# Layer 1's sums begin with rows that GpSimd weighs, and the gate's row is fetched first

## The chip, the cores and the metric

The kernel runs on one core of one Trainium2 chip. The metric is the time of one execution on the device, in microseconds; three executions give the median. Engine names are those of the profile: PE is TensorE, DVE is VectorE, ACT is ScalarE, POOL is GpSimd, SP issues the DMAs.

## The reference

Two layers of a transformer over 1024 tokens (plus 256 context tokens in layer 0), width 1024. Each layer has a mixer (attention), a projection `w_out`, a gated residual with layer norm, and a squared-ReLU MLP with a second gated residual:

```
x = _layer_norm(DEEPNORM_ALPHA * x + g_a * y, ln1_g[l], ln1_b[l])
x = _layer_norm(DEEPNORM_ALPHA * x + g_m * _squared_relu_mlp(x * (1 + sc_m) + sh_m, mlp_w1[l], mlp_w2[l]),
                ln2_g[l], ln2_b[l])
```

So the MLP's sum of a row starts from ALPHA times the normalised, weighted and shifted row: `ALPHA * (xhat * ln1_g + ln1_b)`. The gate `g_a` is one row of 1024 numbers for all tokens (and another for the context).

## The kernel before

`stage_block(layer)` holds projection, first norm and MLP of one layer. Tokens are in tiles of 128: ten in layer 0, eight in layer 1 (`final`). Each engine has its own instruction list and works it off in order; semaphores tie the lists together.

**Projection.** For each tile PE makes 48 matmuls (L2250 to L2252: each fp32 product is three products of split halves) into a pair of PSUM banks. DVE then multiplies by the gate row (L2077, two halves), adds the residual (L2084), takes moments (L2087, L2090), and normalises (L2096); ACT gives the square root between. PE transposes the normalised tile (L2235) after the sixth of the eight k-steps of the *next* tile, so it stands still if the normalised tile is late. In layer 1 the residual tile `r_xin` is x-hat of layer 0's end, and POOL first multiplies it by `r_lng` and adds `r_lnb` (L1972, L1974); L2084 waits for that (`s_past`). In layer 0 POOL's use of these two rows (L1979, L1981) is behind the transposes. SP issues, once the split of `w_out` is done: `r_lng`, `r_lnb` (L1788), the gate row or rows (L1790), the first residual tiles (L1776), then the next `r_raw`. The two rows and the gate rows count on one semaphore `s_row` (three transfers in layer 1, four in layer 0), and both POOL and DVE wait for all of them.

**Start of layer 1's MLP.** The MLP runs in steps of 256 hidden columns. In a step PE makes the first product for two groups of 512 tokens (L2295 to L2297, two column blocks m each), ACT takes ReLU and square (L1947, L1949), POOL squares the ReLU in full precision (L2000), DVE makes the low half (L2163). One step later PE makes the second product (L2273 to L2275) and DVE adds it to the sum `y` (L2106). In layer 1 POOL also multiplies the second weights by the MLP's gate (L1993) and makes the low half of the next first weights (L1987), ACT and DVE split the second weights (L1940, L2156). Before any sum, `begin_y` loads row tile t of `y` (the stored x-hat) and makes it `ALPHA*(y*ln1_g + ln1_b)` by two DVE operations, L2039 and L2041; `r_over` are the two broadcast rows `ln1`. Tile 0 is begun before the split of the last transposed tile (L2025, which PE needs for group 1), tiles 1 to 7 in step 0's second group. PE's wait for the first second product is

```
wait(pe, s_y, tiles + nth(c, t) - 1)
```

With `tiles` = 8 and c = t = 0 that is 7: seven row tiles must be begun, and for t = 1 all eight. PE also waits there for the low halves of group 0 and of the second weights.

Of the kernel before, what the change touches and what calls it, by code (L numbers as in the profile page):

```python
# [19 lines left out]
P = 128  # L20
# [1633 lines left out]
def stage_block(nc, io, k, layer):  # L1654
# [30 lines left out]
    rsem = lambda n: k.sem(f"{rtag}_{n}")  # L1685
    s_row, s_xr, s_past, s_begin = rsem("rows"), [rsem(f"x{i}") for i in range(XB)], rsem("past"), rsem("begin")
    s_raw = [rsem(f"raw{i}") for i in range(2)]
    s_whigh, s_wlow, s_high, s_low, s_yps = [rsem(x) for x in ("whigh", "wlow", "high", "low", "yps")]
    s_dve, s_std, s_g, s_b, s_tr, s_mod, s_hh, s_hl, s_half = [rsem(x) for x in ("dve", "std", "g", "b", "tr", "mod", "hh", "hl", "half")]
    s_lnr, s_lnt, s_fold = rsem("lnr"), rsem("lnt"), rsem("fold")  # L1690
    s_store = [rsem(f"store{i}") for i in range(2)]
# [67 lines left out]
    with nc.Block() as block:  # L1759
        @block.sync  # L1760
        def _(sp):
# [22 lines left out]
            for i, name in enumerate(("ln1_g", "ln1_b")):  # L1784
                sp.dma_start(lnr[i * KT:(i + 1) * KT, :], io[name][layer].rearrange("(k p) -> k p", p=P)).then_inc(s_lnr, 16)
            sp.wait_ge(s_wlow, KT)
            for t, name in ((lng, "ln2_g"), (lnb, "ln2_b")) if final else ((lng, "ln1_g"), (lnb, "ln1_b")):
                sp.dma_start(t[:, :], bass.AP(tensor=io[name].tensor, offset=0, ap=[[0, P], [1, D]])).then_inc(s_row, 16)  # L1788
            for c in range(3 - XB):
                sp.dma_start(rgate[:, c, :].rearrange("p (j q) -> p j q", q=P),  # L1790
                             bass.AP(tensor=k.gate_dram.tensor, offset=(layer * 2 * 2 * KT + c) * P, ap=[[0, P], [2 * P, KT], [1, P]])).then_inc(s_row, 16)
            for t in range(XB):
                residual_in(t)
            for t in range(tiles):
                if t + 2 < tiles:
# [170 lines left out]
        def _(pool):  # L1966
            k.clear_last(pool)
            pool.wait_ge(s_row, 48 if final else 64)
            for t in range(tiles) if final else ():
# [5 lines left out]
            for t in () if final else range(tiles):  # L1975
# [5 lines left out]
                pool.tensor_tensor(r, r, lnb[:, :], ALU.add).then_inc(s_b, 1)  # L1981

            def step(c):
                for m in range(M):
                    if not starts(c):
                        wait(pool, s_ahigh, M * c + m + 1)
                        pool.tensor_tensor(wal[:, m, :, :], rawa[:, m, :, :], f32(wah[:, m, :, :]), ALU.subtract).then_inc(s_alow, 1)  # L1987
                if final:
                    for m in range(M):
                        if starts(c):  # L1990
                            pool.wait_ge(s_grow, 16)
                        wait(pool, s_rawb[m], 16 * (c + 1))
                        pool.tensor_tensor(rawb[:, m, :], rawb[:, m, :], growt, ALU.mult).then_inc(s_bg, 1)  # L1993
                for g, (a, n) in enumerate(groups):
                    for m in range(M):
                        j = J * c + g * M + m
                        wait(pool, s_relu, j + 1)
                        wait(pool, s_atl, j - 1)
                        r = rel[:, m % 2, 0:n]
                        pool.tensor_tensor(sq[:, m % 2, 0:n], r, r, ALU.mult).then_inc(s_sq, 1)  # L2000
                    if ends(c) and not final:
                        for t in (range(4), range(4, 6), range(6, tiles))[g]:
# [11 lines left out]
        def _(dve):  # L2014
# [17 lines left out]
            def begin_y(first, end):  # L2032
                for t in range(first, end):
                    if final:
                        dve.wait_ge(s_yx[t], 16)
                        y = by_j(k.y[:, t, :])
                        if t == 0:
                            dve.wait_ge(s_begin, 32)
                        dve.scalar_tensor_tensor(out=y, in0=y, scalar=ALPHA, in1=ln1[0], op0=ALU.mult, op1=ALU.mult).then_inc(s_past, 1)  # L2039
                        dve.wait_ge(s_past, 2 * tiles + t + 1)  # L2040
                        dve.scalar_tensor_tensor(out=y, in0=ln1[1], scalar=ALPHA, in1=y, op0=ALU.mult, op1=ALU.add).then_inc(s_y, 1)  # L2041
                    else:
# [18 lines left out]

            dve.wait_ge(s_row, 48 if final else 64)
            for t in range(tiles):
# [7 lines left out]
                if t >= 2:  # L2071
                    dve.wait_ge(s_store[t % 2], 16 * (t // 2))
                    dve.wait_ge(s_tr, t - 1)
                dve.wait_ge(s_yps, t + 1)
                for half in range(2):
# [66 lines left out]
            def step(c):  # L2142
# [6 lines left out]
                for g, (a, n) in enumerate(groups):  # L2149
# [3 lines left out]
                    if g == NG - 1:  # L2153
                        for m in range(M):
                            wait(dve, s_bhigh, M * c + m + 1)
                            dve.tensor_tensor(wbl[:, m, :], rawb[:, m, :], f32(wbh[:, m, :]), ALU.subtract).then_inc(s_blow, 1)  # L2156
                        if final and starts(c):
                            begin_y(1, tiles)
                    for m in range(M):
                        j = J * c + g * M + m  # L2160
                        wait(dve, s_sq, j + 1)
                        wait(dve, s_ath, j + 1)
                        dve.tensor_tensor(atl[:, m, a:a + n], sq[:, m % 2, 0:n], f32(ath[:, m, a:a + n]), ALU.subtract).then_inc(s_atl, 1)  # L2163
            def ending_first(c):
                def low(g, m):
# [232 lines left out]
```

## Time and profile before

| | us |
|---|---|
| median of 3 runs | 2968.99 |
| lowest, highest | 2968.83, 2974.59 |
| profiled execution, device time | 2971.22 |
| its span, first to last instruction | 2969.4 |
| PE busy (share of the span) | 2793.5 (94%) |
| DVE, ACT, POOL busy | 1367.4, 887.6, 533.5 |
| mean granted clock of TensorE | 0.973 |

PE is the bound: a wait of PE is time lost, a wait of another engine costs only where PE waits for it in turn. In the rows, "idle before" with an arrow names what ended the idle time. A duration of DVE or POOL includes the time in which the operation has started but makes no progress. The projection of layer 0 begins at about 499 us of the span, that of layer 1 at about 2117 us, layer 1's MLP at about 2229 us.

### The profile page before, as it was taken

How to read it: one execution, taken by the hardware profiler on the slowest of the kernel's cores; microseconds unless marked ns; L12 is line 12 of the kernel's file. 1: busy time of each engine (PE TensorE's matmuls, PEld its weight loads, DVE VectorE, ACT ScalarE, POOL GpSimd, SP SyncE). 2: the span in 40 equal slices, each digit the busy share in tenths (PEclk: the TensorE clock that was granted, in tenths of full speed). 3: DMA queues.
4: the chain of work that ended last, by engine and by line, in shares of the span. 5: the costliest groups of instructions: out<-in, count | busy, mean ns of one | idle time of the engine just before them, and what ended most of it. 6: DMA issues, size and time to landing. Idle time of an engine off the chain costs nothing. (4 is left out here: it accounts for less than half of the span.)

```text
span 2969.4 us, 40552 instructions
## 1 busy us (share of the span) xinstructions
PE 2793.5 (94%) x15615; PEld 2289.2 (77%) x15615; DVE 1367.4 (46%) x2195; ACT 887.6 (30%) x1598; POOL 533.5 (18%) x365
## 2 busy tenths in 40 slices
PE   6999996999999999999969999999697999999998
PEld 3666785788888888888858888888585888888886
DVE  3575554663333333333573565555556333333336
ACT  3244653441211211211132443444342211221222
POOL 0000000341121121111320000000133323323321
PEclk8999998999999999999989999999898999999999
DMA  7584216440010110110331111100455111111112
GB/s 260 189 309 149 75 63 225 123 133 29 29 56 28 39 46 28 42 42 28 85 114 50 36 44 37 36 29 15 129 141 149 57 42 42 57 42 42 57 42 57
DMA packets 202132, 237.42 MB, mean 80 GB/s; under 512 B 15960, under 2 KB 165088, under 8 KB 195872
## 3 DMA queue, kind: packets, MB, share of 16 engines
q1 hardware_dynamic: 201728, 235.74, 24.9%
q8 instruction: 78, 1.28, 0.2%
q14 instruction: 38, 0.31, 0.0%
q10 hardware_dynamic: 288, 0.10, 0.0%
HBM read 203.20 MB, written 36.83 MB: 81 GB/s over the span
## 5 line engine op out<-in xcount | busy, mean ns | idle before, releaser
L2106 DVE TENSOR_TENSOR y<-y,pair 128x1024 f32<-128x1024 f32 x280 | 341.7, 1221 | 337.4 <-PE pair L2275 337.4
L2273 PE MATMUL pair<-m_wbh,m_ath 128*128 128x512 f32 x1080 | 422.1, 391 | 16.8 <-DVE y L2041 16.8
L2275 PE MATMUL pair<-m_wbh,m_atl 128*128 128x512 f32 x1080 | 423.2, 392 | 0.0
L2274 PE MATMUL pair<-m_wbl,m_ath 128*128 128x512 f32 x1080 | 422.2, 391 | 0.0
L1947 ACT ACTIVATE m_rel<-pair 128x512 f32<-128x512 f32 x160 | 88.9, 556 | 1021.0 <-PE pair L2297 1009.9
L2163 DVE TENSOR_TENSOR m_atl<-m_sq,m_ath 128x512 fp32r<-128x512 f32 x150 | 96.4, 644 | 623.1 <-POOL m_sq L2000 623.1
L2000 POOL TENSOR_TENSOR m_sq<-m_rel 128x512 f32<-128x512 f32 x160 | 155.5, 972 | 1124.7 <-ACT m_rel L1947 1124.5
L2297 PE MATMUL pair<-hth,m0n_wal 128*128 128x512 f32 (+1 forms) x768 | 272.2, 354 | 0.0
L2296 PE MATMUL pair<-htl,m0n_wah 128*128 128x512 f32 (+1 forms) x768 | 272.1, 354 | 0.0
L2295 PE MATMUL pair<-hth,m0n_wah 128*128 128x512 f32 (+1 forms) x768 | 271.6, 354 | 0.0
L2273 PEld LDWEIGHTS pair<-m_wbh,m_ath 128*128 128x128 f32 x1080 | 203.4, 188 | 60.7 <-issue 16.3
L2275 PEld LDWEIGHTS pair<-m_wbh,m_atl 128*128 128x128 f32 x1080 | 203.3, 188 | 43.3
L2274 PEld LDWEIGHTS pair<-m_wbl,m_ath 128*128 128x128 f32 x1080 | 203.3, 188 | 43.2
L2295 PE MATMUL pair<-hth,m1n_wah 128*128 128x512 f32 x512 | 200.0, 391 | 3.3 <-DVE htl L2025 3.3
L2296 PE MATMUL pair<-htl,m1n_wah 128*128 128x512 f32 x512 | 200.4, 391 | 0.0
L2297 PE MATMUL pair<-hth,m1n_wal 128*128 128x512 f32 x512 | 200.4, 391 | 0.0
L2296 PEld LDWEIGHTS pair<-htl,m0n_wah 128*128 128x128 f32 x768 | 145.1, 189 | 21.6
L2295 PEld LDWEIGHTS pair<-hth,m0n_wah 128*128 128x128 f32 x768 | 145.1, 189 | 21.1
L2297 PEld LDWEIGHTS pair<-hth,m0n_wal 128*128 128x128 f32 x768 | 145.1, 189 | 20.1
L1496 DVE CUSTOM_DVE_ANT_0 a_sx<-pair,a_tab 128x640 f32<-128x640 f32 (+1 forms) x128 | 96.0, 788 | 86.7 <-PE pair L1588 86.7
L2250 PE MATMUL pair<-r_wh,r_cath 128*128 128x512 f32 x288 | 116.5, 404 | 6.1 <-DVE r_catl L2020 5.0
L1940 ACT ACTIVATE m_wbh<-m_rawb 128x1024 fp32r<-128x1024 f32 x60 | 60.3, 1053 | 194.7 <-PE pair L2275 194.7
(284 smaller groups left out, 5283.7 us busy)
## 6 DMA issues: line engine op xcount, KB each, us to landing
a_ring<-in_w_mod SPq DMA_DIRECT2D x40, 1024.0 KB, 9.4
m_rawb<-in_mlp_w SPq DMA_DIRECT2D x64, 512.0 KB, 4.4
m_rawa<-in_mlp_w SPq DMA_DIRECT2D x60, 512.0 KB, 4.1
x_rows<-r_res SPq DMA_DIRECT2D x26, 512.0 KB, 5.4
r_raw<-cat_cols SPq DMA_DIRECT2D x18, 512.0 KB, 6.4
mod_w<-in_w_mod SPq DMA_DIRECT2D x8, 1024.0 KB, 12.2
r_xin<-in_x SPq DMA_DIRECT2D x16, 512.0 KB, 12.4
gate_pre<-a0g_gout SPq DMA_DIRECT2D x20, 256.0 KB, 2.0
```

The costliest lines, as they stand in the source:

```text
L1496: dve.tensor_tensor_reduce(sx[:, n % 2, hh, 0:keys], two[:, at:at + keys], table(hh, t), -1.0, 3.0e38, ALU.add, ALU.min, sm[:, 0:1]).then_ ...
L1947: act.activation(rel[:, m % 2, 0:n], k.bank[4 + jj % NB1][:, 0:n], ACT.Relu).then_inc(s_relu, 1)
L2000: pool.tensor_tensor(sq[:, m % 2, 0:n], r, r, ALU.mult).then_inc(s_sq, 1)
L2106: dve.tensor_tensor(k.y[:, t, :], k.y[:, t, :], k.pair[t % 2][:, :], ALU.add).then_inc(s_y, 1)
L2163: dve.tensor_tensor(atl[:, m, a:a + n], sq[:, m % 2, 0:n], f32(ath[:, m, a:a + n]), ALU.subtract).then_inc(s_atl, 1)
L2250: pe.matmul(o, cath[:, t % 2, kt, :], wh[:, kt, n], start=kt == 0, stop=False)
L2273: pe.matmul(o, ath[:, m, ts], bh[:, m, cols], start=m == 0, stop=False)
L2274: pe.matmul(o, ath[:, m, ts], bl[:, m, cols], start=False, stop=False)
L2275: i = pe.matmul(o, atl[:, m, ts], bh[:, m, cols], start=False, stop=m == M - 1)
L2295: pe.matmul(o, wah[:, m, kt, :], xh, start=kt == 0, stop=False)
L2296: pe.matmul(o, wah[:, m, kt, :], xl, start=False, stop=False)
L2297: i = pe.matmul(o, wal[:, m, kt, :], xh, start=False, stop=kt == KT - 1)
```

## The change

It has two parts.

**The fetches.** SP issues the gate row of condition 0 first, then the first residual tile, then `r_lng` and `r_lnb`, then the rest. The gate rows have semaphores of their own (`s_rg`). DVE no longer waits for `s_row`; it waits for the gate row at each tile, right before L2077. POOL waits for `r_lng` and `r_lnb` (and in layer 1 for the residual tile, as before).

**The begin of layer 1's sums.** The product `y * ln1_g` of all eight tiles goes from DVE to POOL (`weigh`): tiles 0 to 2 at the start of step 0, ahead of POOL's products of the second weights; tiles 3 and 4 behind its second square, tile 5 behind the third, 6 and 7 behind the fourth. DVE multiplies the row `ln1_b` by ALPHA once, and keeps one operation per tile, `ALPHA*y + that row`. Its tiles 1 to 4 now stand behind group 0's low halves and ahead of the split of the second weights, tiles 5 to 7 behind group 1's low halves. What PE waits for is not changed.

```diff
             sp.wait_ge(s_wlow, KT)
+            gate_in(0)
+            residual_in(0)
             for t, name in ((lng, "ln2_g"), (lnb, "ln2_b")) if final else ((lng, "ln1_g"), (lnb, "ln1_b")):
                 sp.dma_start(t[:, :], ...).then_inc(s_row, 16)
-            for c in range(3 - XB):
-                sp.dma_start(rgate[:, c, :]..., ...).then_inc(s_row, 16)
-            for t in range(XB):
+            for t in range(1, XB):
                 residual_in(t)
+            for c in range(1, 3 - XB):
+                gate_in(c)
...
-            pool.wait_ge(s_row, 48 if final else 64)
+            pool.wait_ge(s_row, 32)
...
+            def weigh(t):
+                if t == 0:
+                    pool.wait_ge(s_begin, 32)
+                pool.wait_ge(s_yx[t], 16)
+                y = by_j(k.y[:, t, :])
+                pool.tensor_tensor(y, y, ln1[0], ALU.mult).then_inc(s_past, 1)
...
+                if starts(c) and final:
+                    for t in range(3):
+                        weigh(t)
...
                         pool.tensor_tensor(sq[:, m % 2, 0:n], r, r, ALU.mult).then_inc(s_sq, 1)
+                        if starts(c) and final:
+                            for t in ((), (3, 4), (5,), (6, 7))[g * M + m]:
+                                weigh(t)
...
-                        dve.wait_ge(s_yx[t], 16)
                         y = by_j(k.y[:, t, :])
                         if t == 0:
                             dve.wait_ge(s_begin, 32)
-                        dve.scalar_tensor_tensor(out=y, in0=y, scalar=ALPHA, in1=ln1[0], op0=ALU.mult, op1=ALU.mult).then_inc(s_past, 1)
+                            dve.tensor_scalar(ln1[1], ln1[1], ALPHA, None, ALU.mult).then_inc(s_shift, 1)
+                            dve.wait_ge(s_shift, 1)
                         dve.wait_ge(s_past, 2 * tiles + t + 1)
-                        dve.scalar_tensor_tensor(out=y, in0=ln1[1], scalar=ALPHA, in1=y, op0=ALU.mult, op1=ALU.add).then_inc(s_y, 1)
+                        dve.scalar_tensor_tensor(out=y, in0=y, scalar=ALPHA, in1=ln1[1], op0=ALU.mult, op1=ALU.add).then_inc(s_y, 1)
...
-            dve.wait_ge(s_row, 48 if final else 64)
...
+                dve.wait_ge(s_rg[cond(t)], 16)
                 dve.wait_ge(s_yps, t + 1)
...
-                        if final and starts(c):
-                            begin_y(1, tiles)
...
+                    if final and starts(c):
+                        begin_y(*((1, 5), (5, tiles))[g])
```

POOL's row at the start of layer 1's MLP before; the first line is the last residual tile, L1987 opens step 1:

```order
L1974 TENSOR_TENSOR r_xin<-r_xin,r_lnb 128x1024
L1993 TENSOR_TENSOR m_rawb<-m_rawb,y 128x1024 x2
L2000 TENSOR_TENSOR m_sq<-m_rel 128x512 x4
L1736 UNCONDITIONAL_BRANCH
L1736 ISA
L1987 TENSOR_TENSOR m1n_wal<-m_rawa,m1n_wah 128x1024
```

The same place after the change (L1994 is the weighing, L2009 the gated weights, L2016 the square, L2000 the low half of step 1):

```order
L1980 TENSOR_TENSOR r_xin<-r_xin,r_lnb 128x1024
L1994 TENSOR_TENSOR y<-y,r_over_15488 128x1024 x3
L2009 TENSOR_TENSOR m_rawb<-m_rawb,y 128x1024 x2
L2016 TENSOR_TENSOR m_sq<-m_rel 128x512 x2
L1994 TENSOR_TENSOR y<-y,r_over_15488 128x1024 x2
L2016 TENSOR_TENSOR m_sq<-m_rel 128x512
L1994 TENSOR_TENSOR y<-y,r_over_15488 128x1024
L2016 TENSOR_TENSOR m_sq<-m_rel 128x512
L1994 TENSOR_TENSOR y<-y,r_over_15488 128x1024 x2
L1737 UNCONDITIONAL_BRANCH
L1737 ISA
L2000 TENSOR_TENSOR m1n_wal<-m_rawa,m1n_wah 128x1024
```

Eight operations of 128x1024 have come into POOL's row ahead of step 1, three of them ahead of the gated weights and the first square.

DVE's row before, from the last tile's normalisation on (L2025 is the split of the last transposed tile, L2163 the low halves, L2156 the split of the second weights); six more pairs L2039, L2041 follow, then L2163 twice:

```order
L2096 TENSOR_SCALAR r_res<-r_res,r_mv,r_rstd 128x1024
L2039 SCALAR_TENSOR_TENSOR y<-y,r_over_15476 128x1024
L2041 SCALAR_TENSOR_TENSOR y<-r_over_15476,y 128x1024
L2025 TENSOR_TENSOR htl<-r_modt,hth 128x8x128
L2163 TENSOR_TENSOR m_atl<-m_sq,m_ath 128x512 x2
L2156 TENSOR_TENSOR m_wbl<-m_rawb,m_wbh 128x1024 x2
L2039 SCALAR_TENSOR_TENSOR y<-y,r_over_15476 128x1024
```

DVE's row after, up to the end of step 0:

```order
L2115 TENSOR_SCALAR r_res<-r_res,r_mv,r_rstd 128x1024
L2057 TENSOR_SCALAR r_over_15488<-r_over_15488 128x8x128
L2060 SCALAR_TENSOR_TENSOR y<-y,r_over_15488 128x1024
L2044 TENSOR_TENSOR htl<-r_modt,hth 128x8x128
L2180 TENSOR_TENSOR m_atl<-m_sq,m_ath 128x512 x2
L2060 SCALAR_TENSOR_TENSOR y<-y,r_over_15488 128x1024 x4
L2175 TENSOR_TENSOR m_wbl<-m_rawb,m_wbh 128x1024 x2
L2180 TENSOR_TENSOR m_atl<-m_sq,m_ath 128x512 x2
L2060 SCALAR_TENSOR_TENSOR y<-y,r_over_15488 128x1024 x3
```

Sixteen begin operations have become eight and one scaling; four of them now stand ahead of the split of the second weights, and the last three behind both remaining low halves.

SP's row in layer 0 before, from the norm's weights to the third cat tile:

```order
L1785 DMA r_lnr<-in_ln_b 8x128
L1788 DMA r_lng<-in_ln_g 128x1024
L1788 DMA r_lnb<-in_ln_b 128x1024
L1790 DMA r_gate<-gate_rows 128x8x128 x2
L1776 DMA r_xin<-in_x 128x1024
L1766 DMA r_raw<-cat_cols 128x8x128
```

The same after:

```order
L1786 DMA r_lnr<-in_ln_b 8x128
L1789 DMA r_gate<-gate_rows 128x8x128
L1777 DMA r_xin<-in_x 128x1024
L1795 DMA r_lng<-in_ln_g 128x1024
L1795 DMA r_lnb<-in_ln_b 128x1024
L1789 DMA r_gate<-gate_rows 128x8x128
L1767 DMA r_raw<-cat_cols 128x8x128
```

The gate's first row has moved from third to first place, the residual tile from fifth to second. In layer 1 the order changes in the same way, with one gate row and a second residual tile in its place.

## Rows read from the trace of the kernel before

**Rows 1.** The page: busy time and share of the span of each engine
```profile
PE 2793.5 (94%) x15615; PEld 2289.2 (77%) x15615; DVE 1367.4 (46%) x2195; ACT 887.6 (30%) x1598; POOL 533.5 (18%) x365
```

**Rows 2.** Waits of PE, 2105 to 2300 us (us in all, times, longest)
```profile
PE pair L2273 <- DVE y L2041: 16.8, 2, 15.9
PE pair L2235 <- DVE r_res L2096: 11.9, 2, 11.0
...
PE pair L2295 <- DVE htl L2025: 3.3, 1, 3.3
```

**Rows 3.** Timeline of POOL, 2138 to 2152 us (start, us, operation, idle before)
```profile
2140.86 2.34 POOL L1972 TENSOR_TENSOR r_xin<-r_xin,r_lng 128x1024 f32<-128x1024 f32 x1 [81.54 <-DMA r_xin<-x_rows]
...
2145.58 2.34 POOL L1972 TENSOR_TENSOR r_xin<-r_xin,r_lng 128x1024 f32<-128x1024 f32 x1
2147.99 3.20 POOL L1974 TENSOR_TENSOR r_xin<-r_xin,r_lnb 128x1024 f32<-128x1024 f32 x1
```

**Rows 4.** Timeline of DVE, 2138 to 2152 us
```profile
2145.72 3.27 DVE L2084 SCALAR_TENSOR_TENSOR r_res<-r_xin,r_res 128x1024 f32<-128x1024 f32 x1 [5.16 <-POOL r_xin L1974]
```

**Rows 5.** Timeline of DVE, 2238 to 2284 us
```profile
2240.79 1.45 DVE L2039 SCALAR_TENSOR_TENSOR y<-y,r_over 128x1024 f32<-128x1024 f32 x1 [6.00 <-DMA y<-x_rows]
...
2243.41 1.22 DVE L2025 TENSOR_TENSOR htl<-r_modt,hth 128x1024 fp32r<-128x1024 f32 x1
...
2261.66 1.22 DVE L2039 SCALAR_TENSOR_TENSOR y<-y,r_over 128x1024 f32<-128x1024 f32 x1
...
2266.45 3.37 DVE L2039 SCALAR_TENSOR_TENSOR y<-y,r_over 128x1024 f32<-128x1024 f32 x1
...
2276.44 3.28 DVE L2041 SCALAR_TENSOR_TENSOR y<-r_over,y 128x1024 f32<-128x1024 f32 x1
```

**Rows 6.** Timeline of POOL, 2235 to 2280 us
```profile
2236.39 4.76 POOL L1993 TENSOR_TENSOR m_rawb<-m_rawb,y 128x1024 f32<-128x1024 f32 x2 [19.05 <-DMA m_rawb<-in_mlp_w]
...
2258.16 1.24 POOL L2000 TENSOR_TENSOR m_sq<-m_rel 128x512 f32<-128x512 f32 x1 [4.39 <-ACT m_rel L1947]
2265.69 6.33 POOL L1987 TENSOR_TENSOR m1n_wal<-m_rawa,m1n_wah 128x1024 fp32r<-128x1024 f32 x2 [6.28 <-ACT m1n_wah L1923]
2271.98 6.66 POOL L1993 TENSOR_TENSOR m_rawb<-m_rawb,y 128x1024 f32<-128x1024 f32 x2
```

**Rows 7.** Timeline of PE, 2238 to 2284 us
```profile
2244.69 0.69 PE L2295 MATMUL pair<-hth,m1n_wah 128*128 128x512 f32 x1 [3.28 <-DVE htl L2025]
...
2273.33 0.79 PE L2273 MATMUL pair<-m_wbh,m_ath 128*128 128x512 f32 x1 [15.88 <-DVE y L2041]
...
2279.77 0.50 PE L2273 MATMUL pair<-m_wbh,m_ath 128*128 128x512 f32 x1 [0.96 <-DVE y L2041]
```

**Rows 8.** Tile y on SP, 2246.5 to 2249.5 us: issue to landing
```profile
DMA to landing us min/median/max: 5.0/6.6/11.4
```

**Rows 9.** Timeline of DVE, 514 to 524 us
```profile
517.70 1.28 DVE L2077 TENSOR_TENSOR r_res<-pair,r_gate 128x512 f32<-128x512 f32 x2
519.02 1.23 DVE L2084 SCALAR_TENSOR_TENSOR r_res<-r_xin,r_res 128x1024 f32<-128x1024 f32 x1
...
522.37 0.81 DVE L2096 TENSOR_SCALAR r_res<-r_res,r_mv,r_rstd 128x1024 f32<-128x1024 f32 x1
```

**Rows 10.** Timeline of PE, 518 to 530 us
```profile
523.24 1.97 PE L2235 MATMUL pair<-kept_ident,r_res 128*128 128x128 f32 x8 [4.65 <-DVE r_res L2096]
```

**Rows 11.** Windows: us, then PE busy (x), PEld, DVE, ACT, POOL, PEclk, DMA, GB/s
```profile
523.20:527.90 4.70, 4.66 (x15) 4.08 (x16) 1.14 (x1) 2.66 (x8) 2.44 (x2) 0.50 0.41 119
2273.30:2278.80 5.50, 5.47 (x12) 3.84 (x12) 5.46 (x2) 0.00 (x0) 5.34 (x2) 0.50 0.33 94
```

**Rows 12.** Timeline of SP, 505 to 530 us
```profile
507.77 0.36 SPq L1788 DMA_DIRECT2D r_lng<-in_ln_g  x1
```

**Rows 13.** DMA issues, 505 to 530 us (issue to landing in us)
```profile
r_lng<-in_ln_g SPq DMA_DIRECT2D x1, 512.0 KB, 4.5
r_lnb<-in_ln_b SPq DMA_DIRECT2D x1, 512.0 KB, 5.5
```

More of the change, by code:

```diff
@@ L1685, in stage_block @@
     rsem = lambda n: k.sem(f"{rtag}_{n}")
-    s_row, s_xr, s_past, s_begin = rsem("rows"), [rsem(f"x{i}") for i in range(XB)], rsem("past"), rsem("begin")
+    s_row, s_xr, s_past, s_begin, s_shift = rsem("rows"), [rsem(f"x{i}") for i in range(XB)], rsem("past"), rsem("begin"), rsem("shift")
     s_raw = [rsem(f"raw{i}") for i in range(2)]
@@ L1689, in stage_block @@
     s_dve, s_std, s_g, s_b, s_tr, s_mod, s_hh, s_hl, s_half = [rsem(x) for x in ("dve", "std", "g", "b", "tr", "mod", "hh", "hl", "half")]
+    s_rg = [rsem(f"rgate{c}") for c in range(2)]
     s_lnr, s_lnt, s_fold = rsem("lnr"), rsem("lnt"), rsem("fold")
@@ L1786, in _, with gate_in @@
             sp.wait_ge(s_wlow, KT)
+            def gate_in(c):
+                sp.dma_start(rgate[:, c, :].rearrange("p (j q) -> p j q", q=P),
+                             bass.AP(tensor=k.gate_dram.tensor, offset=(layer * 2 * 2 * KT + c) * P, ap=[[0, P], [2 * P, KT], [1, P]])).then_inc(s_rg[c], 16)
+            gate_in(0)
+            residual_in(0)
             for t, name in ((lng, "ln2_g"), (lnb, "ln2_b")) if final else ((lng, "ln1_g"), (lnb, "ln1_b")):
                 sp.dma_start(t[:, :], bass.AP(tensor=io[name].tensor, offset=0, ap=[[0, P], [1, D]])).then_inc(s_row, 16)
-            for c in range(3 - XB):
-                sp.dma_start(rgate[:, c, :].rearrange("p (j q) -> p j q", q=P),
-                             bass.AP(tensor=k.gate_dram.tensor, offset=(layer * 2 * 2 * KT + c) * P, ap=[[0, P], [2 * P, KT], [1, P]])).then_inc(s_row, 16)
-            for t in range(XB):
+            for t in range(1, XB):
                 residual_in(t)
+            for c in range(1, 3 - XB):
+                gate_in(c)
             for t in range(tiles):
```

## The prediction

> **What bounds the kernel now.** I read the page's busy shares first: PE is busy for 94% of the span and no other engine for half of it [rows 1]. So a change outside PE counts only by the waits of PE that it shortens or makes. Next PE's waits around layer 1's block [rows 2]: the longest of the stretch is 15.9 us for the begun sums (L2041, with a second of 0.96 us for the eighth tile), then 11.0 us for the first normalised tile, then 3.3 us for the split of the last transposed tile. In layer 0 PE waits 4.65 us for the first normalised tile [rows 10]. The change touches the first two of these places and the last.
>
> Then I looked at what DVE and POOL do while PE waits 15.9 us. DVE runs one begin operation behind another, and the same form takes 1.22 us at 2261.66 but 3.37 us at 2266.45 [rows 5]. The long ones begin where POOL starts its work for step 1: two low halves in 6.33 us and two gated weights in 6.66 us [rows 6], where the same gated weights took 4.76 us for two when DVE was idle. From 2266.45 to 2279.72 DVE got four operations done and POOL, within the same 13.27 us, about four. That is 3.32 us for one operation of each. POOL alone needs 2.38 us for one and DVE about 1.2: the two take turns, nothing runs side by side. The first tile shows the order of turns: POOL starts its next product at 2145.58, DVE's L2084 at 2145.72 takes 3.27 us, until 2148.99, and POOL's next, started at 2147.99, takes 3.20 us in its turn [rows 3, 4]. Sums that read PSUM are not among these operations.
>
> The Trainium skill has the rule for this in "SBUF — State Buffer", section "Who interferes with whom": a DVE instruction with two SBUF inputs and a GpSimd instruction that reads SBUF exclude each other, and whoever issued first holds the port for its whole length. It speaks against this change, which moves work to the engine that holds the port twice as long, and the trace agrees. What it leaves open is who comes next where both have a queue; rows 5 and 6 show turns. If POOL kept the port through its whole queue instead, DVE would start later, but the sum below is of all operations and would be no smaller.
>
> **Part 1, the fetches, layer 0.** The transfers of SP's queue land one after another: the first issued at 507.77 lands 4.5 us later, at 512.3; the second, issued some 0.4 us behind it, takes 5.5 us and lands near 513.7 [rows 12, 13]. All are of 512 KB. The gate row takes the first place and the residual tile the second, so L2077 can start near 512.5 and L2084 near 513.9. Before, L2077 starts at 517.70, L2084 at 519.02, and L2096 ends at 522.37 + 0.81 = 523.18 [rows 9]: 4.16 us from the start of L2084. The same chain now ends near 513.9 + 4.2 = 518.1. PE comes to the transposes at 523.24 - 4.65 = 518.6 [rows 10]. The wait goes: 4.65 us. Behind it the clock is at 0.50 (its lower level, 1.2 GHz) for 4.7 us [rows 11]; if PE never stands still it should not fall, and at full clock this stretch takes half: another 2.35 us. Sum 7.0 us. What is late next is the third cat tile, the sixth transfer in both orders: at 1.4 to 1.5 us per place it lands near 520, is split by ACT and DVE in about 2.3 us, and PE, through with the second tile at about 518.6 + 0.9 + 12 x 0.23 = 522.3, comes to it just then. I leave it at nothing. Two rows for POOL, `r_lng` and `r_lnb`, land later, but POOL first uses them behind the transposes. Bounds: if the gate's row lands one place later (1.4 us), PE waits about 1 us and gains 3.6 us without the clock; 7.0 is the other end.
>
> **Part 1, layer 1.** Here DVE's L2084 waits for POOL, and POOL needs the residual tile and both rows. These are four transfers with the gate's row, and the last of the four lands when it did: POOL starts at 2140.86 [rows 3]. The gate's product is earlier but L2084 waits 5.16 us for POOL [rows 4]. So the 11.0 us stay. Nothing, within 0.5 us either way.
>
> **Part 2, the begin of the sums.** Removed: eight DVE operations of 128x1024. Added: eight POOL operations of that size, at 2.38 us alone, and one scaling on DVE, at most as long as L2096 (0.81), hidden in the 6.00 us in which DVE waits for the first stored tile [rows 5]. PE still needs seven begun tiles. I count what has to go through the shared port before the seventh, from the landing of tile 0 (2240.8):
> - POOL, 128x1024: eight weighings, two gated weights of step 0 (before, these ran at 2236.39, in the gap; now they queue behind three weighings), and, as DVE's list is not through when POOL reaches step 1, two low halves and two gated weights of step 1. 14 operations. At 128x512: four squares.
> - DVE, 128x1024: the split L2025, two of the second weights, seven begins. 10 operations. At 128x512: four low halves.
>
> Ten pairs at 3.32 us are 33.2; four half-size pairs at 1.66 (half of it) are 6.6; the four operations that POOL has over at 2.38 are 9.5. Sum 49.3 us: the seventh tile is begun at 2290.1. The port has no gap on the way: the other five tiles are issued from 2246.44 on, land 5.0 to 11.4 us from their issue [rows 8], and their turns run from 2257 to 2274; the last square's input is there near 2263 (group 1's products took 2273.33 - 15.88 - 2244.69 = 12.8 us [rows 7], now from 2249.8 on), its turn is near 2269. Before, the seventh begin ended at 2266.45 + two pairs = 2273.1 and PE started 0.2 us later, at 2273.33 [rows 5, 7]. Now 2290.3, 17.0 us later. The second wait of 0.96 us [rows 7] goes, since the eighth begin follows one DVE operation later, inside the first tile's 5.5 us at half clock [rows 11]. Cost 16.0 us.
>
> On the way group 1 of PE's first product is late too. It waits for the split of the last transposed tile: weighing 0 until 2243.2, begin 0 in turn behind weighing 1 until 2246.5, the split behind weighing 2 until 2249.8, against 2243.41 + 1.22 = 2244.6. PE's 3.28 us [rows 7] become about 8.4. This does not add to the 16.0, as PE waits for the seventh tile in any case. What is queued behind POOL's weighings is the gated weights, then the squares; for these wait ACT's split of the weights and DVE's low halves, all of it inside the count.
>
> Bounds of this cost: if the five POOL operations that the seventh tile doesn't need (weighing 7, step 1's four) come after it, 11.9 us less: 4.1 us. Above, some 18 us, if a turn takes 2.42 us of POOL rather than 2.38 and each has a gap. I take 16.0, because the turns of rows 5 and 6 are of these very operations.
>
> **Sum.** -7.0 + 0 + 16.0 = +9.0 us. The profiled execution took 2971.22 us for a span of 2969.4; it would be 2980.2. The median of the runs shown is 2968.99, 2.2 us less, so 2978.0 us.
>
> **Rivals.**
> - *The turns let the seventh tile by.* If DVE passes POOL's last five operations, part 2 costs 4.1 us and the sum is -2.9: 2966 us, no change that can be told. For it: POOL's low halves of step 1 wait for weights, and these start only at 2265.69 [rows 6]. Against: that is long before their turn near 2278. 14%.
> - *No exclusion for the weighings.* This is the faster one. Place: step 0's start. If a weighing ran beside DVE's work, POOL alone would have done weighing 6 after 2240.8 + 9 x 2.38 (seven weighings and two gated weights) + 4 x 1.2 (a square, [rows 6]) = 2267.1, the begin ends at 2268.3, PE gains 4.8 + 0.96 us, and with layer 0's 7.0 the sum is -12.8: 2956 us. It decides as soon as DVE's begins take 1.2 us beside POOL's work. Rows 4 and 5 speak against it; for it only that no weighing has run yet. 10%.
> - *Layer 0 gives nothing.* The gate's row lands as small pieces and slow, or PE stands for the third cat tile instead. Then +16.0: 2985 us. The cat tile is not far from the edge (it is the sixth transfer in both orders). 10%.
>
> **How the numbers follow.** The forecast, both terms as worked out, has 66%; its own range is 2973 to 2982. A change within 0.2% (5.9 us) can't be told from none. Slower by more: nearly all of the forecast (0.61) and the third rival (0.10), 0.71. Same: the edge of the forecast (0.05) and the first rival, most of it (0.12), 0.17. Faster: 0.12. The range from 2966 to 2984 takes in the forecast, the first rival and part of the third, and leaves out the faster case.
>
> **What would show it.** Right: weighings of 3.2 to 3.4 us each in the timeline of POOL, begins of about 3.3 us on DVE with no idle time between, PE's first L2273 waiting 25 to 29 us and started near 2283 (7 us earlier by layer 0), PE's wait before group 1 near 8 us; in layer 0 L2235 of the first tile with no wait and the clock at 1.00 behind it; in layer 1's projection the 11.0 us unchanged. Wrong: begins of 1.2 us beside weighings; a wait of PE for L2273 under 16 us; a new wait of PE at layer 0's third tile; a first gate row that lands later than 514.

## The result, and the profile after

The changed kernel takes 2980.37 us (median of 9 runs) against 2970.58 us of the kernel before (9 runs): ratio 1.0031, interval 1.0022 to 1.0040. It is slower by 9.8 us. The forecast was 2978.0 us, +9.0 us.

The page of the changed kernel, first the span, then busy time and share of each engine:

```profile
span 2978.8 us, 40573 instructions
PE 2795.6 (94%) x15615; PEld 2291.0 (77%) x15615; DVE 1376.2 (46%) x2188; ACT 887.4 (30%) x1598; POOL 561.7 (19%) x373
```

PE is busy 2 us more than in [rows 1] and the span is 9.4 us longer, so the loss is waiting. The first and last records of PE's work in each stage cut both spans into the same pieces (start of the piece to start of the next, in us):

| stage | before | after | difference |
|---|---|---|---|
| start to layer 0's first projection product | 498.81 | 498.22 | -0.6 |
| to layer 0's last transposes | 131.81 | 126.01 | -5.8 |
| to layer 1's first projection product | 1486.84 | 1488.80 | +2.0 |
| to layer 1's last transposes | 117.38 | 117.53 | +0.2 |
| to the first second product (L2273, now L2292) | 38.49 | 53.86 | +15.4 |
| to the second tile's | 6.44 | 4.92 | -1.5 |
| to the end | 689.63 | 689.46 | -0.2 |
| sum | 2969.4 | 2978.8 | +9.4 |

The third stage (layer 0's MLP and both attentions) is work that the change doesn't touch. Among the profiles of all twelve kernels of this study it takes 1486.8 to 1488.8 us. The two kernels with the old fetches are at the low end, but so are three with the new ones, so no edit is shown to set it; with one profile per kernel the possibility isn't closed either. The first piece, ahead of every edit, differs even more, from 494.5 to 498.8 us. Differences of one or two us between whole spans of two profiles are therefore not read as an effect here, only those inside a stage.

PE's waits around layer 1's block (line, what it waited for: us in total, times, longest):

```profile
PE pair L2292 <- DVE y L2060: 25.2, 1, 25.2
PE pair L2254 <- DVE r_res L2115: 11.6, 2, 10.7
PE pair L2314 <- DVE htl L2044: 8.0, 1, 8.0
```

They answer to [rows 2]: the wait for the begun sums is 25.2 us instead of 15.9, that for the first normalised tile is 10.7 instead of 11.0, that for the last transposed tile's split is 8.0 instead of 3.3. POOL in that stretch (start, us, engine, line, out<-in, count of instructions; L1994 is the weighing, L2009 the gated weights, L2016 the squares, L2000 step 1's low half):

```profile
2236.05 7.94 POOL L1994 TENSOR_TENSOR y<-y,r_over 128x1024 f32<-128x1024 f32 x3 [22.84 <-DMA y<-x_rows]
2243.95 5.70 POOL L2009 TENSOR_TENSOR m_rawb<-m_rawb,y 128x1024 f32<-128x1024 f32 x2
2249.61 2.03 POOL L2016 TENSOR_TENSOR m_sq<-m_rel 128x512 f32<-128x512 f32 x2
2251.61 5.64 POOL L1994 TENSOR_TENSOR y<-y,r_over 128x1024 f32<-128x1024 f32 x2
2257.21 2.02 POOL L2016 TENSOR_TENSOR m_sq<-m_rel 128x512 f32<-128x512 f32 x1
2259.19 3.34 POOL L1994 TENSOR_TENSOR y<-y,r_over 128x1024 f32<-128x1024 f32 x1
2262.48 2.02 POOL L2016 TENSOR_TENSOR m_sq<-m_rel 128x512 f32<-128x512 f32 x1
2264.47 6.59 POOL L1994 TENSOR_TENSOR y<-y,r_over 128x1024 f32<-128x1024 f32 x2
2271.02 6.06 POOL L2000 TENSOR_TENSOR m1n_wal<-m_rawa,m1n_wah 128x1024 fp32r<-128x1024 f32 x2
2277.04 6.06 POOL L2009 TENSOR_TENSOR m_rawb<-m_rawb,y 128x1024 f32<-128x1024 f32 x2
```

No row but the first has idle time before it: from the landing of tile 0 at 2236.05 POOL works to 2283.10 without a gap. DVE beside it (L2060 begin, L2044 split of the transposed tile, L2180 low halves, L2175 split of the second weights):

```profile
2238.52 3.27 DVE L2060 SCALAR_TENSOR_TENSOR y<-y,r_over 128x1024 f32<-128x1024 f32 x1 [7.42 <-POOL y L1994]
2241.72 3.35 DVE L2044 TENSOR_TENSOR htl<-r_modt,hth 128x1024 fp32r<-128x1024 f32 x1
2250.68 4.32 DVE L2180 TENSOR_TENSOR m_atl<-m_sq,m_ath 128x512 fp32r<-128x512 f32 x2 [5.61 <-POOL m_sq L2016]
2254.92 10.66 DVE L2060 SCALAR_TENSOR_TENSOR y<-y,r_over 128x1024 f32<-128x1024 f32 x4
2265.51 6.63 DVE L2175 TENSOR_TENSOR m_wbl<-m_rawb,m_wbh 128x1024 fp32r<-128x1024 f32 x2
2272.06 5.57 DVE L2180 TENSOR_TENSOR m_atl<-m_sq,m_ath 128x512 fp32r<-128x512 f32 x2
2277.55 7.77 DVE L2060 SCALAR_TENSOR_TENSOR y<-y,r_over 128x1024 f32<-128x1024 f32 x3
```

In turn with a POOL operation of its own size, a DVE operation of 128x1024 takes about 3.3 us, as in [rows 5]. The four begins in 10.66 us are two such turns and two beside a square of half the size, 2.06 us each. The last begin of the last group starts when POOL is through and takes 1.2. PE's rows for the two waits, and its granted clock in the first tile of the second product and behind it (window, length, busy of PE, PEld, DVE, ACT, POOL, PEclk, DMA share, GB/s):

```profile
2245.12 0.79 PE L2314 MATMUL pair<-hth,m1n_wah 128*128 128x512 f32 x1 [8.00 <-DVE htl L2044]
2284.42 0.79 PE L2292 MATMUL pair<-m_wbh,m_ath 128*128 128x512 f32 x1 [25.23 <-DVE y L2060]
```

```profile
2284.40:2288.30 3.90, 3.88 (x9) 3.12 (x10) 0.92 (x1) 0.00 (x0) 0.00 (x0) 0.50 0.00 0
2288.30:2292.00 3.70, 3.70 (x16) 2.98 (x16) 1.22 (x1) 0.00 (x0) 0.00 (x0) 0.92 0.00 0
```

As in [rows 11], PE starts at 1.2 GHz (clock 0.50) after the wait. The second tile's first product follows at 2289.34 with no wait, so [rows 7]'s 0.96 us is gone.

In layer 0 the first tile's chain on DVE (L2096 the gate, L2103 the residual, L2115 the normalisation, L2039 the split of the third cat tile, that is of PE's input for the third tile, fetched from `cat_cols`) and PE's transposes and third tile:

```profile
511.66 1.29 DVE L2096 TENSOR_TENSOR r_res<-pair,r_gate 128x512 f32<-128x512 f32 x2 [1.40 <-DMA r_gate<-gate_rows]
513.22 1.23 DVE L2103 SCALAR_TENSOR_TENSOR r_res<-r_xin,r_res 128x1024 f32<-128x1024 f32 x1 [0.27 <-DMA r_xin<-in_x]
516.57 0.81 DVE L2115 TENSOR_SCALAR r_res<-r_res,r_mv,r_rstd 128x1024 f32<-128x1024 f32 x1
520.43 2.08 DVE L2039 TENSOR_TENSOR r_catl<-r_raw,r_cath 128x1024 fp32r<-128x1024 f32 x1 [3.04 <-ACT r_cath L1880]
```

```profile
517.81 1.03 PE L2254 MATMUL pair<-kept_ident,r_res 128*128 128x128 f32 x8
522.65 0.47 PE L2269 MATMUL pair<-r_wh,r_cath 128*128 128x512 f32 x1 [1.06 <-DVE r_catl L2039]
```

The 4.65 us of [rows 10] are gone and the clock of 500 to 545 us is 1.00 where it was 0.92. In their place stands 1.06 us for the third cat tile. In layer 1 DVE's L2103 still waits for POOL (8.80 us, until 2141.01), and POOL for the last of its transfers, as in [rows 3, 4]:

```profile
2136.14 2.35 POOL L1978 TENSOR_TENSOR r_xin<-r_xin,r_lng 128x1024 f32<-128x1024 f32 x1 [81.38 <-DMA r_lnb<-in_ln_b]
```

### The profile page after: what moved, and what is told of

Its sections match the earlier page's. It is cut to its first block and busy times, and to the rows that moved or that the text cites. A ratio compares the mean times of both kernels' runs of the same rounds, so it can differ in the third digit from the quotient of the medians.

```text
span 2978.8 us, 40573 instructions
## 1 busy us (share of the span) xinstructions
PE 2795.6 (94%) x15615; PEld 2291.0 (77%) x15615; DVE 1376.2 (46%) x2188; ACT 887.4 (30%) x1598; POOL 561.7 (19%) x373
## 5 line engine op out<-in xcount | busy, mean ns | idle before, releaser
L2292 PE MATMUL pair<-m_wbh,m_ath 128*128 128x512 f32 x1080 | 422.0, 391 | 25.2 <-DVE y L2060 25.2
L2180 DVE TENSOR_TENSOR m_atl<-m_sq,m_ath 128x512 fp32r<-128x512 f32 x150 | 103.6, 692 | 624.4 <-POOL m_sq L2016 624.4
L2016 POOL TENSOR_TENSOR m_sq<-m_rel 128x512 f32<-128x512 f32 x160 | 157.1, 983 | 1116.0 <-ACT m_rel L1953 1115.9
L2292 PEld LDWEIGHTS pair<-m_wbh,m_ath 128*128 128x128 f32 x1080 | 203.3, 188 | 68.4 <-issue 25.7
L2314 PEld LDWEIGHTS pair<-hth,m1n_wah 128*128 128x128 f32 x512 | 96.9, 189 | 29.1 <-DVE htl L2044 8.4
```

The source lines that it names most:

```text
L2292: pe.matmul(o, ath[:, m, ts], bh[:, m, cols], start=m == 0, stop=False)
L2314: pe.matmul(o, wah[:, m, kt, :], xh, start=kt == 0, stop=False)
```

## The experiments

Ten kernels, with 4 to 11 runs each beside the kernel before (medians 2970.0 to 2970.1 us in all three batches). Brackets are 95% intervals of the ratio. What was to be told apart: the two parts and whether they add; port against a mere queue; and where a better version lies.

**One part each.** The first kernel holds only the fetches, the second only POOL's weighings with DVE's new order of begins. The edits are the two halves of the diff above.

> Only the fetches (gate row first, residual tile second, gate waited for alone); the begin of layer 1's sums as before. Theory (the two parts add, the fetches help): in layer 0 the wait of 4.65 us for the first normalised tile goes, with the half clock behind it, less a wait of about 1 us for the third cat tile, as in the trace after: about 5.6 us faster, ratio 0.998. In layer 1's projection the 11 us stay. Rival (the gain of layer 0 is given back later): within 2 us of before, ratio 0.9995 or more.

> Only the weighing on POOL, with DVE's new order; the fetches as before. Theory (DVE and POOL take turns at a shared port, and all of the work goes through it): from the landing of stored tile 0 to PE's first second product 48.4 us as in the trace after, against 32.5 before, about 15 us slower than before, ratio 1.005. Rival (the two parts interact, and the weighing alone costs what the pair cost): about 9.8 us slower, ratio 1.0033.

The fetches alone take 2965.7 us, ratio 0.9987 [0.9978, 0.9996]: -4.3 us. The weighings alone take 2983.51 us, 1.0038 [1.0025, 1.0052]: +13.5 us. In us the intervals are -6.5 to -1.2 and +7.4 to +15.4. The sum of the two medians, +9.2, is the change's +9.8 within them: they add. PE's wait in the second kernel, in the first's place of [rows 2]:

```profile
PE pair L2286 <- DVE y L2054: 28.4, 1, 28.4
PE pair L2308 <- DVE htl L2038: 5.5, 1, 5.5
```

**A begin that doesn't read its second operand from SBUF.** If the port is the cause, a begin whose row comes from PSUM should pass POOL's work; if only POOL's list is too long, nothing changes.

```diff
-  dve.scalar_tensor_tensor(out=y, in0=y, scalar=ALPHA, in1=ln1[1], ...)
+  dve.scalar_tensor_tensor(out=y, in0=y, scalar=ALPHA, in1=by_j(k.pair[1][:, :]) if t else ln1[1], ...)
```

> The changed kernel, but the begins of tiles 1 to 7 add a PSUM tile instead of the row of ln1_b, so that each has one SBUF input only; this leaves out the shift of these rows. POOL's list is the same. Theory (turns at a port that only operations with two SBUF inputs and POOL use): a begin takes about 1.2 us beside a weighing, a weighing 2.4 to 2.6 us; seven begins leave the port, about 7 us of it before the seventh tile is begun; PE's first second product comes about 41 us after the landing of tile 0 instead of 48.4, so 6 to 8 us faster than the changed kernel, about 2973. Rival (POOL's longer queue alone is the cause, whatever DVE does): 48 us as before this edit, same time as the changed kernel, about 2980. A third: PSUM operands share the turns too, begins of 3.3 us and no change.

This kernel leaves out the row of `ln1_b` for seven tiles and adds whatever stands in that PSUM pair, so its output is of no use and only its time says something. 2967.03 us, 0.9988 [0.9979, 0.9997]: 3.0 us under before, where the changed kernel is 9.8 over, so 12.8 us less. DVE's begins, and PE's start:

```profile
2254.91 4.60 DVE L2060 SCALAR_TENSOR_TENSOR y<-y,pair 128x1024 f32<-128x1024 f32 x4
2269.04 3.47 DVE L2060 SCALAR_TENSOR_TENSOR y<-y,pair 128x1024 f32<-128x1024 f32 x3
```

```profile
2271.61 0.79 PE L2292 MATMUL pair<-m_wbh,m_ath 128*128 128x512 f32 x1 [13.03 <-DVE y L2060]
```

Four begins now take 4.60 us instead of 10.66, three 3.47 instead of 7.77, and the weighing beside the first four (2258.21) takes POOL's own 2.35. POOL's list is the same, and PE starts 35.6 us after tile 0's landing (2236.05 here too) instead of 48.4. So it is the exclusion, and "POOL's list alone" falls. Of a DVE instruction with at most one SBUF input, outside its 2-port modes, the section of the Trainium skill that the forecast quotes ("SBUF — State Buffer", "Who interferes with whom") says that it does not contend with GpSimd; the trace agrees, with four begins in 4.60 us. I had the size too small by half. The trace gives it: the seven begins take 10.36 us less (4.60 + 3.47 for 10.66 + 7.77), and the split of the second weights between them 4.20 instead of 6.63 us, 2.43 less, since it now runs beside the end of a weighing and a square. Together 12.8. I had priced the begins and not what stands behind them.

**The other way round: no weighings, begins earlier on DVE.** The last tile's split first, then the begins of tiles 0 to 2 at once instead of behind step 0's first products.

```diff
-            begin_y(0, 1 if final else XT)
-            split_ht(tiles - 1)
+            if final:
+                split_ht(tiles - 1)
+                begin_y(0, 3)
...
-                            begin_y(1, tiles)
+                            begin_y(3, tiles)
```

> The fetches, and no weighing on POOL: both begin operations stay on DVE, but the split of the last transposed tile goes ahead of begin 0, and tiles 1 and 2 are begun right behind it, in the time in which DVE stands idle before the first low half; tiles 3 to 7 as before. Theory (the seventh begin sets PE's start, and what counts is to have DVE's begins done before POOL reaches step 1 at about 2264): the seventh begin ends about 20 to 22 us after the landing of tile 0 instead of 32.5, PE starts 10 to 12 us earlier; with the fetches' 5.6 about 16 us faster than before, near 2955, ratio 0.9948. Rival (DMA landings of tiles 3 to 7 or the stores bound the begins): the gain beyond the fetches is under 5 us, 2960 to 2965.

2963.58 us, 0.9975 [0.9966, 0.9984]: -6.4 us, of which the fetches are 4.3. Much less than I expected. DVE:

```profile
2233.99 3.33 DVE L2031 TENSOR_TENSOR htl<-r_modt,hth 128x1024 fp32r<-128x1024 f32 x1 [5.21 <-ACT hth L1893]
2261.87 3.28 DVE L2047 SCALAR_TENSOR_TENSOR y<-r_over,y 128x1024 f32<-128x1024 f32 x1
2265.07 5.64 DVE L2173 TENSOR_TENSOR m_atl<-m_sq,m_ath 128x512 fp32r<-128x512 f32 x2
```

The split runs beside POOL's gated weights and takes 3.33 us, so that PE still waits 2.0 us for it; and the last begins and the last two low halves still meet POOL's step 1 (its low halves run from 2261.08 on). PE's wait for the sums falls from 15.9 to 10.8 us, and a new one comes behind it, for the first sum, which stands behind those low halves on DVE:

```profile
2260.93 0.79 PE L2283 MATMUL pair<-m_wbh,m_ath 128*128 128x512 f32 x1 [10.77 <-DVE y L2047]
2271.90 0.50 PE L2283 MATMUL pair<-m_wbh,m_ath 128*128 128x512 f32 x1 [2.96 <-DVE y L2116]
```

The size is that of my rival, but not its reason: no begin waited for a landing. DVE has no idle time from 2233.99 on, and the seventh begin ends at 2260.70, before POOL's step 1. So up to PE's start it is DVE's own list that counts, two operations per tile, and behind it the turns. What I missed is that DVE's whole list must be through before POOL starts step 1, not only the begins.

**The begin moved out of the stretch.** Where POOL has time is layer 1's projection: busy 19.74 of 48 us. There it can make `ALPHA*(y*ln1_g + ln1_b)` of each normalised tile in place, after PE's transposes and before the store, so that the row comes back as the begun sum. The first form does both operations on POOL; the second leaves the addition to DVE, one operation per tile (split first, tiles 0 to 2 early).

```diff
+            def row(t):                       # POOL, layer 1's projection
+                r = by_j(res[:, t % 2, :])
+                pool.wait_ge(s_dve, C * t + 6)
+                pool.wait_ge(s_tr, t + 1)
+                pool.tensor_tensor(r, r, ln1[0], ALU.mult).then_inc(s_g, 1)
+                pool.wait_ge(s_g, t + 1)
+                pool.tensor_tensor(r, r, ln1[1], ALU.add).then_inc(s_b, 1)   # first form only
...
+                        dve.tensor_tensor(y, y, ln1[1], ALU.add).then_inc(s_y, 1)   # second form only
```

> The fetches, and no begin at the MLP's start at all: during the projection, where POOL is busy for a fifth of the time, it multiplies each normalised tile by ALPHA*ln1_g and adds ALPHA*ln1_b behind its transposes (as it does in layer 0), the stored rows are the begun sums, and DVE only waits for their landing. Theory (the wait of 15.9 us is made of port work between the landing of the rows and step 1; taken from there it is gone): PE has no wait for begun sums, starts step 1 some 15 us earlier; POOL's added work takes turns with DVE in the projection, which may cost up to 1 us per tile in waits for L2096. About 2955, between 2950 and 2960, ratio 0.995. Rival (turns in the projection eat it): waits of PE for the normalised tiles of over 10 us more in all, 2962 or above.

> As e5_rows, but POOL only multiplies in the projection (one operation per tile), and DVE adds the row ALPHA*ln1_b at the MLP's start, one operation per tile, tiles 0 to 2 ahead of the first low half. Theory: half the port work at the MLP's start and half in the projection; PE still waits for the seventh begin, which ends about when its row lands (20 us after the landing of tile 0), so about 2957 to 2961, 2 to 5 us behind e5_rows. Rival (the projection is so near its limit that the second POOL operation costs more than the begins): faster than e5_rows.

The first takes 2957.91 us, 0.9960 [0.9947, 0.9974]: -12.1 us. The second takes 2951.23 us, 0.9932 [0.9918, 0.9945]: -18.8 us. So the order of the two is the other way round than I expected (the second 2 to 5 us behind the first): the rival named there came true. Cut into the pieces of the table above, the first form gains 20.0 us behind the last transposes (18.5 instead of 38.5) and loses 10.6 in layer 1's projection (128.0 instead of 117.4); the second gains 14.0 and loses 1.1. The fetches and the order of DVE's begins are the same in the second form as in the kernel with the early begins, which is at 0.9975; what moving the product alone brings is the rest, about 12 us.

The same 48 us of the projection in the first, in the second and (shifted by 5 us) in the kernel before:

```profile
2165.00:2213.00 48.00, 43.87 (x204) 35.78 (x203) 37.81 (x39) 18.89 (x39) 41.83 (x16) 1.00 0.40 111
```

```profile
2165.00:2213.00 48.00, 48.00 (x230) 40.05 (x229) 33.49 (x40) 21.69 (x47) 32.97 (x13) 1.00 0.52 143
```

```profile
2170.00:2218.00 48.00, 48.00 (x230) 40.03 (x229) 29.62 (x42) 21.73 (x45) 19.74 (x9) 1.00 0.56 160
```

With two operations per tile POOL is busy for 41.83 of the 48 us, DVE's operations queue for the port and PE stands for 4 of them; with one PE never stands. PE's waits of the first form and of the second:

```profile
PE pair L2259 <- DVE r_res L2118: 21.0, 8, 11.0
```

```profile
PE pair L2255 <- DVE r_res L2112: 12.8, 3, 11.7
PE pair L2293 <- DVE y L2053: 6.1, 1, 6.1
```

In the first form even the normalisation, which has one SBUF input of data, waits for POOL, 2.68 us instead of 0.81, in five of the eight tiles. One of them:

```profile
2226.11 2.68 DVE L2118 TENSOR_SCALAR r_res<-r_res,r_mv,r_rstd 128x1024 f32<-128x1024 f32 x1
```

**The 11 us of layer 1's projection.** The gate's row was never what ended it. This kernel has the fetches of the change, but in layer 1 the first residual tile comes first, then both rows, then the gate's row, and DVE scales the first tile itself; in layer 0 the third cat tile is fetched ahead of the norm's rows.

```diff
+            if not final:
+                cat_in(2)
...
+                if t == 0 and final:
+                    dve.wait_ge(s_row, 32)
+                    dve.wait_ge(s_xr[0], 16)
+                    x = xres[:, 0, :]
+                    dve.tensor_tensor(x, x, lng[:, :], ALU.mult).then_inc(s_own, 1)
+                    dve.wait_ge(s_own, 1)
+                    dve.tensor_tensor(x, x, lnb[:, :], ALU.add).then_inc(s_own, 1)
```

> e1_fetch, and for the first tile: in layer 1 the order is residual tile, its two rows, gate row, and DVE, which stands idle there, multiplies and adds for tile 0 instead of POOL; in layer 0 the third cat tile is fetched ahead of the two rows that POOL needs late. Theory: in layer 1 the 11 us wait shortens by one transfer (2.1 us), by 2.3 us of operations (two DVE instead of two POOL) and by the 2.2 us turn that L2084 loses to POOL: 5 to 6 us; in layer 0 the 1.06 us wait for the third cat tile goes. About 6 us faster than e1_fetch, 2959 to 2961. Rival (another transfer or the table of POOL's second tile becomes the bound): under 2 us faster than e1_fetch.

2958.13 us, 0.9962 [0.9948, 0.9975]: 7.6 us less than the fetches alone. The first tile's chain no longer has POOL's two operations in it and its L2106 meets no turn of POOL's (1.23 us, not 3.27). PE's wait is 4.8 us, where it is 12.8 in the profile of the fetches alone, 10.7 in the changed kernel and 11.0 before:

```profile
2130.66 1.23 DVE L2087 TENSOR_TENSOR r_xin<-r_xin,r_lng 128x1024 f32<-128x1024 f32 x1 [4.59 <-DMA r_lnb<-in_ln_b]
2134.38 1.23 DVE L2106 SCALAR_TENSOR_TENSOR r_res<-r_xin,r_res 128x1024 f32<-128x1024 f32 x1
```

```profile
PE pair L2257 <- DVE r_res L2118: 5.7, 2, 4.8
```

What the third cat tile is worth can be read in layer 0, where this kernel differs from the one with a single multiplication only by that fetch. PE comes to the first transposes 20.9 us into the projection in both; the other then waits 1.07 us for the third cat tile, this one doesn't, and the stage takes 126.0 instead of 127.4 us. So 1.4 of the 7.6 us are layer 0's, and the rest is the first tile's chain; the order of the fetches and DVE's two operations were not run apart.

**Together.** The order of the last kernel with each of the two forms before it.

> e5_rows and e7_first together. If they add: about 2949. If not (the first tile and the rows compete for the same transfers and turns): no better than e5_rows.

> e6_one and e7_first together: POOL's single multiplication in the projection, DVE's single addition at the MLP's start, and the first tile by DVE with the transfers in that order. The two shorten different waits, so they should add: e6_one is 18.8 us under before, e7_first 7.6 us under e1_fetch, which gives 26 us, about 2944, ratio 0.991. Rival: they share the transfers at the start, and it is no better than e8_all (2949.9).

With the first form 2949.89 us, 0.9925 [0.9911, 0.9938], 8.0 us under that form alone. With the second 2939.98 us, 0.9903 [0.9888, 0.9918]: 30.1 us under the kernel before (24.4 to 33.3 by the interval) and 40 under the changed one, the lowest median of the study; 26 us were expected from adding the two. What is left of the two waits:

```profile
PE pair L2309 <- DVE y L2060: 7.4, 1, 7.4
PE pair L2271 <- DVE r_res L2128: 5.8, 2, 4.9
```

**Is the wait for the begins needed at all?** PE's second product doesn't read `y`; only DVE's sum does. Here PE no longer waits for the begins, and DVE waits for all of them ahead of its first sum.

```diff
-                        dve.tensor_tensor(y, y, ln1[1], ALU.add).then_inc(s_y, 1)
+                        dve.tensor_tensor(y, y, ln1[1], ALU.add).then_inc(s_begun, 1)
...
+                            dve.wait_ge(s_begun, XT)
```

> e9_best, and PE no longer waits for seven and eight begins before the first two second products; only DVE waits for all begins before its first sum. Theory: PE's wait of 6.1 us for the seventh begin moves behind the second tile and becomes a wait for the first sum, which DVE can make at about the end of its low halves; what is gained is the two tiles' time less a longer half clock, 1 to 4 us under e9_best. Rival: the wait only changes its name, within 1 us of e9_best.

2943.28 us (4 runs), 0.9903 [0.9888, 0.9918]: not to be told from the kernel without the edit, whose median is 3.3 us lower at the same ratio. The gain of 1 to 4 us did not come; the rival did. PE starts two tiles (at 2242.58) and stands at the third, whose banks the first sum must free; DVE makes that sum only at 2251.50, behind its last begin, which waited for the last stored tile, and its low halves:

```profile
PE pair L2313 <- DVE y L2145: 4.4, 1, 4.4
```

```profile
2249.03 1.23 DVE L2060 TENSOR_TENSOR y<-y,r_over 128x1024 f32<-128x1024 f32 x1 [0.93 <-DMA y<-x_rows]
2251.50 2.34 DVE L2145 TENSOR_TENSOR y<-y,pair 128x1024 f32<-128x1024 f32 x2
```

The wait changed its name; the landing of the last stored tile and DVE's list behind it set it in both.

## Why the prediction was right

**The sum.** +9.0 us forecast, +9.8 [+6.5, +11.9] measured, and both terms of it have their own run.

**Layer 0: 7.0 forecast, 5.8 in the trace, 4.3 (1.2 to 6.5) in the run of that part alone.** The wait of 4.65 us and the half-clock stretch went as said (4.65 + 2.35). What came back is 1.06 us for the third cat tile, which I had named as next in line and set at nothing. It isn't nothing because the tile's split on DVE took 2.08 us, not 1.2 (it ran beside POOL's first product, started at 519.02), and because PE came for it at 521.59, not 522.3: the transposes started at 517.81, for which I had 518.6. The landing, at 519.33, was not late.

The 4.3 us of the single part are not apart from 5.8, as the interval shows, and its profile can't explain them: that execution took 2970.05 us, the longest of eleven with a median of 2965.7. What the profiles do show is that the gain depends on PE's clock at the start of the projection. In every kernel PE first stands for 7 to 10 us, runs ten matmuls, which begin at 0.50, and then stands 1.7 to 2.7 us for its first split. In some profiles the clock is at 1.00 when it goes on and stays there, in others it is at 0.50 for a part of the next 6 us. In the profiles of before and of the changed kernel the clock of 500 to 505 us is 1.00, in those of the two single parts 0.75 and 0.70. A PE that starts slower reaches the first tile's transposes later and waits less for them: 3.3 us in the kernel with the weighings alone, which has the old fetches, against 4.65. With the new fetches it then has no wait for the third cat tile. So like is to be compared with like: with the fast start the stage takes 131.8 us with the old fetches and 126.0 with the new ones, with a start of over 5 us at 0.50 it takes 132.4 (weighings alone) and 127.4 to 127.5 (begins from PSUM, fetches alone). The fetches are worth 5.8 us in the first case and 5.0 in the second. Which start the timed executions had is not known.

**Layer 1's projection: 0 forecast, +0.2 in the trace.** The wait is 10.7 instead of 11.0 us, and its end is POOL's, as [rows 3, 4] had it. The reordered kernel, with 4.8 us, shows that those transfers and POOL's operations together were the cause. From profile to profile this wait is not steady: with the same order of fetches it is 12.8 us in the one of the fetches alone, so "within 0.5 us" was too narrow.

**The begins: +16.0 forecast, 15.4 - 1.5 = 13.9 in the trace, +13.5 in the run of that part alone.** Steps that held: the weighings run without a gap from tile 0's landing; 14 operations of 128x1024 and 4 of 128x512 on POOL before the seventh begin is through; turns of 3.3 us for a pair of full size; PE's wait before group 1 8.0 us (8.4 forecast); its wait for L2292 25.2 (25 to 29 forecast); start at 2284.4 (2283 forecast); the second wait gone. The term that was mis-sized is the count of port time: 49.3 us forecast from the landing to the seventh begin, 48.1 measured (2236.05 to about 2284.1). The count of operations is right; about 0.7 of the 1.2 us are the four squares, 1.03 us each where the forecast's pairs hold 1.2. Another 0.5 us is the first tile's length, 4.92 us instead of 5.48, and a further 0.5 us that transposes and landing lie 5.5 us apart here, 5.95 before.

So the mechanism and the sizes held, but that the total is within 0.8 us is in part luck: layer 0 gave 1.2 us less than forecast and part 2 cost 2.1 us less, which nearly cancel, and the untouched stage between them was 2.0 us longer in this profile, for which no cause is shown. The medians of the single parts sum to +9.2.

**Rivals.** *The turns let the seventh tile by* fell: step 1's four POOL operations (2271.02 to 2283.10) ran in turns with DVE's last low halves and begins, before the seventh. *No exclusion for the weighings* fell by the same rows, and the begins that read PSUM show what the exclusion costs: 12.8 us of the changed kernel's time. That kernel is only 3.0 us faster than before, where this rival had 12.8, because its splits and low halves still take turns with POOL. *Layer 0 gives nothing* fell by the run of the fetches alone, though its interval reaches down to 1.2 us.

**What stays open.** Who gets the port next was only seen as turns; whether another order of the two lists would let DVE pass was not tried. What sets the level of PE's clock at the start of layer 0's projection was not tested, nor why the stage between the two projections takes up to 2.0 us more in some profiles.

## What to carry to other kernels

Where DVE and POOL both have lists of two-input SBUF work, count the operations of both together: a pair costs nearly the sum of both, here 3.3 us for 1.2 and 2.38, and moving one of DVE's two operations per tile to POOL made the stretch longer (+13.5 us). Move such work instead to a stretch where both have room, and count there too: the same product made by POOL in the projection before gave -18.8 us with the fetches and the earlier begins (about 12 of it its own), while two operations per tile filled POOL and gave only -12.1. When a wait is for several transfers, the order of the fetches helps only for the ones that the first user really needs: 4 to 6 us in layer 0, nothing in layer 1, where the gain came when the order and the work behind those transfers were changed together.

## What the runs showed of the hardware that I had not expected

- An operation of DVE with one input in SBUF and one in PSUM runs at its full pace beside POOL's 128x1024 products: 1.2 us each, with POOL's 2.35 us unchanged. The same operation with both in SBUF took 3.3.
- The normalisation (TENSOR_SCALAR, one SBUF input of data, 128x1024 in 0.81 us) did wait for POOL: 2.68 us, in five tiles of the kernel with both operations in the projection and in six of the one that adds the reordered start. That it reads one input doesn't free it.
- POOL's squares of 128x512 in turn with DVE's operations of 128x1024 took 2.02 us each, where two without took 2.03 together, so half-size operations pay for the turns too.
- PE's clock behind one and the same short wait is not the same from profile to profile, though the ten matmuls ahead of the wait begin at 0.50 in all of them: the windows below are of 500 to 505 us, in layer 0's projection, of the changed kernel and of the fetches alone (window, length, busy of PE, PEclk, DMA share, GB/s). It moves the wait behind it by about 1.4 us (4.65 against 3.3) and the gain of removing that wait by 0.8 (5.8 against 5.0).

```profile
500.00:505.00 5.00, 5.00 (x24) 1.00 0.00 0
```

```profile
500.00:505.00 5.00, 5.00 (x18) 0.75 0.00 0
```
